# First attention of a two-block transformer kernel: a head's short score units, its combinations and its exponentials moved; the last head reordered; meta scores 128 wide in the second attention

## What is computed

```python
def diff_attention(q1, q2, k1, k2, v, lam, q_chunk_blocks, k_chunk):
    def block(args):
        qb1, qb2, qc = args
        mask = k_chunk[None, :] <= qc[:, None]
        def probs(qb, k):
            s = jnp.einsum('bqhd,bkhd->bhqk', qb, k).astype(jnp.float32) * scale
            return jax.nn.softmax(jnp.where(mask, s, -jnp.inf), axis=-1)
        a = probs(qb1, k1) - lam * probs(qb2, k2)
        return jnp.einsum('bhqk,bkhd->bqhd', a.astype(v.dtype), v)
...
    o = rms_norm(o, g_sub) * (1.0 - lam_init)
    return h + o.reshape(B, L, H * DIFF_V_DIM) @ w_o
```

## Time and profile before

| | |
|---|---|
| median of 3 runs | 2028.45 us (2028.07 to 2030.13) |
| time of the profiled execution | 2028.63 us |
| its span, first to last instruction | 2026.8 us |
| PE busy | 2009.0 us, 99% |
| DVE, ACT, POOL busy | 1317.6, 852.0, 1164.9 us |
| granted TensorE clock | 0.999 of full speed (2.4 GHz) |
| first attention, heads 0 to 7, about | 30 to 251 us of the span |
| second attention, about | 718 to 863 us |

### The profile page before, as it was taken

One profiled execution on the slowest core, in us unless ns is written; L12 is line 12 of the kernel. 1 busy time (PEld: TensorE's weight loads), 2 busy tenths in 40 slices (PEclk: granted clock), 3 DMA queues, 4 the chain that ended last, 5 costly groups with the idle time before them and its releaser, 6 DMA issues.

```text
span 2026.8 us, 37421 instructions
## 1 busy us (share of the span) xinstructions
PE 2009.0 (99%) x13376; PEld 1804.8 (89%) x13376; DVE 1317.6 (65%) x2199; ACT 852.0 (42%) x1499; POOL 1164.9 (57%) x1395
## 2 busy tenths in 40 slices
PE   9999999999999999999999999999999999999998
PEld 9999899999999988899999998777788888988987
DVE  7777757857746868757857778865512457857654
ACT  5444434433423577634433425344422234433433
POOL 6445356675757522146675767744455557766765
PEclk9999999999999999999999999999999999999999
DMA  5222122232233311122232323322223223232322
GB/s 190 84 74 72 53 85 92 84 117 92 92 97 115 94 34 42 32 89 94 67 131 94 104 94 105 104 84 83 74 93 103 84 84 95 83 125 83 125 83 84
DMA packets 51986, 183.06 MB, mean 90 GB/s; under 512 B 5648, under 2 KB 7824, under 8 KB 51856
## 3 DMA queue, kind: packets, MB, share of 16 engines
q1 hardware_dynamic: 50304, 178.87, 27.3%
q10 hardware_dynamic: 1552, 2.42, 0.4%
HBM read 179.17 MB, written 2.10 MB: 89 GB/s over the span
## 4 chain that ended last, share of the span: by engine, by line
PE 93%; DVE 4%; issue 1%; ACT 1%; POOL 1%; DMA 0%; DVEq 0%; ACTq 0%; SPq 0%
PE ps L805 25%; PE ps L806 24%; PE ps L807 24%; PE ps L929 3%; PE ps L930 3%; PE ps L931 3%; PE ps L1180 2%; PE ps L1197 1%; PE ps L1190 1%; PE ps L1090 1%; PE ps L1121 1%; POOL w_lo L759 1%; PE ps L1105 0%; PE ps L1191 0%; PE ps L1407 0%
## 5 line engine op out<-in xcount | busy, mean ns | idle before, releaser
L739 POOL TENSOR_TENSOR w_lo<-w_raw,w_hi 128x256 fp32r<-128x256 f32 x1140 | 964.1, 878 | 744.5 <-ACT w_hi L2256 735.9
L805 PE MATMUL ps<-x_hi,w_hi 128*128 128x264 f32 (+2 forms) x2504 | 823.0, 329 | 0.0
L806 PE MATMUL ps<-x_lo,w_hi 128*128 128x264 f32 (+2 forms) x2504 | 813.5, 325 | 0.0
L807 PE MATMUL ps<-x_hi,w_lo 128*128 128x264 f32 (+2 forms) x2504 | 812.3, 324 | 0.0
L805 PEld LDWEIGHTS ps<-x_hi,w_hi 128*128 128x128 f32 x2504 | 471.3, 188 | 49.6 <-issue 5.4
L806 PEld LDWEIGHTS ps<-x_lo,w_hi 128*128 128x128 f32 x2504 | 470.8, 188 | 42.1 <-issue 0.2
L807 PEld LDWEIGHTS ps<-x_hi,w_lo 128*128 128x128 f32 x2504 | 471.3, 188 | 39.6
L2256 ACT ACTIVATE w_hi<-w_raw 128x1024 fp32r<-128x1024 f32 x267 | 278.0, 1049 | 72.1 <-PE ps L807 56.4
L805 PE MATMUL ps<-g_hi,w_hi 128*128 128x264 f32 (+3 forms) x648 | 207.9, 321 | 1.0 <-DVE g_lo L1916 1.0
L806 PE MATMUL ps<-g_lo,w_hi 128*128 128x264 f32 (+3 forms) x648 | 205.9, 318 | 0.0
L807 PE MATMUL ps<-g_hi,w_lo 128*128 128x264 f32 (+3 forms) x648 | 205.6, 317 | 0.0
(11 more groups left out here) (278 smaller groups left out, 3044.1 us busy)
## 6 DMA issues: line engine op xcount, KB each, us to landing
w_raw<-stream SPq DMA_DIRECT2D x334, 512.0 KB, 3.5
h<-x_t SPq DMA_DIRECT2D x4, 528.0 KB, 6.7
out_t<-h SPq DMA_DIRECT2D x6, 256.0 KB, 2.3
scratch<-rotary_tables ACTq DMA_DIRECT2D x4, 264.0 KB, 5.4
out_t<-h ACTq DMA_DIRECT2D x2, 256.0 KB, 2.5
par<-params ACTq DMA_DIRECT2D x1, 342.0 KB, 4.7
scratch<-positions ACTq DMA_DIRECT2D x1, 256.0 KB, 2.6
cst<-shape_constants ACTq DMA_DIRECT2D x1, 193.0 KB, 6.2
```

The costliest lines, as they stand in the source:

```text
L739: last = nc.gpsimd.tensor_tensor(w_lo[:, ring(j), cols], w_raw[:, j % 4, cols], w_hi[:, ring(j), cols].bitcast(F32), ALU.subtract)
L805: nc.tensor.matmul(out_ap, w_hi[:, s, c], xh[:, k, cols], start=first, stop=False)
L806: nc.tensor.matmul(out_ap, w_hi[:, s, c], xl[:, k, cols], start=False, stop=False)
L807: return nc.tensor.matmul(out_ap, w_lo[:, s, c], xh[:, k, cols], start=False, stop=last)
```

## The change

1. PE: `scores` 1 to 4 of head `hd + 1` leave the start of `head_a(hd + 1)` and stand at the end of `head_a(hd)`, ahead of `sub_sum` and `value_transposes`.
2. ACT: `exps(hd + 1, 1)` leaves the start of the next head and stands ahead of `take_values(hd + 1)`.
3. DVE: `combine` and `piece_a` stand ahead of the norm step of the same idx. The order at the end of the head (`maximum` 0, p5, `take_output` 4, `combine` 0) is kept.
4. Last head: other order of `wo_blocks`, `sub_sum` and, on DVE and ACT, of norms and copies; `sub_sum` uses banks 2 and 5. `tile_pair` gets `held=1`, so only the last block of both tiles is left for it (before: one block of the first and two of the second).
5. Second attention: unit 4's scores take 128 query columns instead of 16 as stationary operand. The other 112 rows of the result aren't read.

```diff
@@ tile_pair
-                        for b in range(blocks - 1 - m, blocks):
+                        for b in range(blocks - (held if m else 1), blocks):
@@ scores_of_b
-                s = scores_b(idx)
+                s = scores_b(idx) if t else ps[:, 4, UNIT_COLS[2] + UNIT_COLS[3]:UNIT_COLS[2] + UNIT_COLS[3] + META]
...
-                    last = nc.tensor.matmul(s[:, k0:k1], q_b[rows, h % 4, q0:q0 + nq], k_b[rows, h % 4, k0:k1],
+                    last = nc.tensor.matmul(s[:, k0:k1], q_b[rows, h % 4, q0:q0 + P], k_b[rows, h % 4, k0:k1],
@@ PE head_a
-                for idx in range(1, 5):
-                    step(scores, idx)
                 for idx in range(5):
...
+                for idx in range(1, 5):
+                    scores(hd + 1, 1 - par_, idx)
                 if sums:
-                    sub_sum(hd - 1, 1 - par_, 0, 6 * hd + 11)
+                    sub_sum(hd - 1, 1 - par_, (0, 1), 6 * hd + 11)
                 value_transposes(hd + 1, 1 - par_)
@@ PE last_head_a
-                for idx in range(1, 5):
-                    scores(hd, par_, idx)
                 transposes(hd, par_, 0)
-                sub_sum(HEADS_A - 2, 0)
+                pe.wait_ge(ln_done, N_SUB + HEADS_A - 2)
+                wo_blocks(0, 0, 0, 5)
                 values(hd, par_, 0)
+                pe.wait_ge(exp_done, 5 * hd + 2)
+                sub_sum(HEADS_A - 2, 0, (2, 5))
                 transposes(hd, par_, 1)
-                pe.wait_ge(ln_done, N_SUB + HEADS_A - 1)
-                wo_blocks(0, 0, 0, 5)
+                wo_blocks(0, 1, 0, 5)
                 values(hd, par_, 1)
                 transposes(hd, par_, 2)
-                wo_blocks(0, 1, 0, 5)
+                wo_blocks(0, 0, 5, 6), wo_blocks(0, 1, 5, 6)
                 values(hd, par_, 2)
                 transposes(hd, par_, 3)
-                wo_blocks(0, 0, 5, 6), wo_blocks(0, 1, 5, 6)
+                wo_blocks(0, 0, 6, 7), wo_blocks(0, 1, 6, 7)
                 values(hd, par_, 3)
                 transposes(hd, par_, 4)
-                wo_blocks(0, 0, 6, 7), wo_blocks(0, 1, 6, 7)
+                pe.wait_ge(ln_done, N_SUB + HEADS_A - 1)
+                wo_blocks(1, 0, 0, 2)
                 values(hd, par_, 4)
                 pe.wait_ge(exp_done, 5 * HEADS_A)
                 pe.wait_ge(r_ready, N_SUB + HEADS_A - 1)
-                wo_blocks(1, 0, 0, 3)
-                sub_sum(HEADS_A - 1, 1, 4)
-                wo_blocks(1, 0, 3, 6), wo_blocks(1, 1, 0, 6)
+                wo_blocks(1, 0, 2, 6)
+                sub_sum(HEADS_A - 1, 1, (4, 5))
+                wo_blocks(1, 1, 0, 7), wo_blocks(1, 0, 6, 7)
@@ DVE head_a
+                    combine(hd, par_, idx + 1)
+                    piece_a(hd + 1, 1 - par_, idx)
                     if norms and idx < 3:
                         (sub_scale, sub_hi, sub_lo)[idx](hd - 2)
-                    combine(hd, par_, idx + 1)
-                    piece_a(hd + 1, 1 - par_, idx)
                     take_output(hd, par_, idx)
@@ DVE last_head_a
+                combine(hd, par_, 1)
                 sub_scale(hd - 2)
-                combine(hd, par_, 1)
                 take_output(hd, par_, 0)
+                combine(hd, par_, 2)
                 sub_hi(hd - 2), sub_lo(hd - 2)
-                combine(hd, par_, 2)
                 take_output(hd, par_, 1)
+                combine(hd, par_, 3)
                 sub_scale(hd - 1)
-                combine(hd, par_, 3)
                 take_output(hd, par_, 2)
-                sub_hi(hd - 1)
                 combine(hd, par_, 4)
-                sub_lo(hd - 1)
+                sub_hi(hd - 1), sub_lo(hd - 1)
@@ ACT head_a
                 for idx in range(5):
+                    if idx in range(1, 4):
+                        exps(hd, par_, idx + 1)
+                    take_transposed(hd, par_, idx)
                     if idx == 4:
-                        take_transposed(hd, par_, idx)
                         exps(hd + 1, 1 - par_, 0)
-                    else:
-                        exps(hd, par_, idx + 1)
-                        take_transposed(hd, par_, idx)
...
+                exps(hd + 1, 1 - par_, 1)
                 take_values(hd + 1, 1 - par_)
```

More of the change, by code:

```diff
@@ L831, in pair_blocks, with tile_pair @@
                            b == 0, False)
-            def tile_pair(j, tl, blocks, xh, xl, T, ready, begun=False):
+            def tile_pair(j, tl, blocks, xh, xl, T, ready, begun=False, held=2):
                 if not begun:
@@ L845, in tile_pair, with tiles @@
                     last.then_inc(half_done, 1)
-            def tiles(j, tl, n, blocks, xh, xl, T, ready, after_first=None, paired=False, begun=False, T_odd=None):
+            def tiles(j, tl, n, blocks, xh, xl, T, ready, after_first=None, paired=False, begun=False, T_odd=None, held=2):
                 done = 0
@@ L855, in tiles @@
                 if paired:
-                    tile_pair(j, tl, blocks, xh, xl, T, ready, begun)
+                    tile_pair(j, tl, blocks, xh, xl, T, ready, begun, held)
                     done = 2
@@ L872, in norm_sum @@
             def norm_sum(steps, T, src=acc, semaphore=acc_step, bank0=6, pieces=0):
+                banks = bank0 if isinstance(bank0, tuple) else (bank0, bank0 + 1)
                 pe.wait_ge(semaphore, steps)
@@ L876, in norm_sum @@
                     wait(pe, chunk_taken, pieces + bank if not isinstance(pieces, int) or pieces else 0)
-                    last = nc.tensor.matmul(ps[:, bank0 + bank, 0:n], ones[:, :], src[:, t0:t0 + n],
+                    last = nc.tensor.matmul(ps[:, banks[bank], 0:n], ones[:, :], src[:, t0:t0 + n],
                                             start=True, stop=True)
@@ L1244, in head_b, with sub_sum @@
                     output_blocks(1, 1, 0, 6)
-            def sub_sum(n, par_, bank0=0, pieces=0):
+            def sub_sum(n, par_, bank0=(0, 1), pieces=0):
                 pe.wait_ge(r_ready, N_SUB + n)
@@ L1314, in _ @@
             piece_a(0, 5)
+            for idx in range(1, 5):
+                scores(0, 0, idx)
             pe.wait_ge(blocks_clear, 1)
@@ L1325, in _ @@
             last_head_a()
-            tiles(J_WO, TL_WO, KD, KD, g_hi, g_lo, T1, (g_ready, G_WO), paired=True, begun=True)
+            tiles(J_WO, TL_WO, KD, KD, g_hi, g_lo, T1, (g_ready, G_WO), paired=True, begun=True, held=1)
             ffn(J_F0, TL_F0, X_F0, G_F0, T1, N_F0, layer=0)
@@ L2319, in inverse_rms @@
                     act.wait_ge(ss_ready, norm + 1)
-                    src = ps[:, bank0, 0:T2] if T == T2 else ps[:, bank0:bank0 + 2, 0:T // 2]
+                    a, b = bank0 if isinstance(bank0, tuple) else (bank0, bank0 + 1)
+                    src = ps[:, a, 0:T2] if T == T2 else ps[:, a:b + 1:b - a, 0:T // 2]
                 else:
@@ L2460, in sub_square, with sub_rms @@
                 square(o_buf[:, n, :], par_, 0, (o_taken, 5 * n + 5), (ss_ready, N_SUB + n - 1), T1)
-            def sub_rms(n, bank0=0):
+            def sub_rms(n, banks=(0, 1)):
                 wait(act, sub_step, n)
-                inverse_rms(N_SUB + n, P, T1, acc, bank0)
+                inverse_rms(N_SUB + n, P, T1, acc, banks)
             def head_a(hd, par_, j, i=0):
@@ L2489, in last_head_a @@
                 hd, par_ = HEADS_A - 1, 1
-                exps(hd, par_, 1)
                 take_transposed(hd, par_, 0)
[L2492 to L2495, removed]
+                exps(hd, par_, 2)
+                sub_rms(hd - 1, (2, 5))
+                take_transposed(hd, par_, 1)
+                exps(hd, par_, 3)
+                take_transposed(hd, par_, 2)
+                exps(hd, par_, 4)
+                take_transposed(hd, par_, 3)
                 take_transposed(hd, par_, 4)
@@ L2611, in _ @@
             hi_part(6)
+            exps(0, 0, 1)
             take_values(0, 0)
@@ L2621, in _ @@
             sub_square(HEADS_A - 1, 1)
-            sub_rms(HEADS_A - 1, 4)
+            sub_rms(HEADS_A - 1, (4, 5))
             residual(J_WO, TL_WO, T1, N_F0)
```

## The result

| | before | after |
|---|---|---|
| median of the timed runs | 2028.3 us | 2056.3 us |
| span of the profiled execution | 2026.8 us | 2055.7 us |
| PE busy | 2009.0 us | 2018.6 us |
| granted TensorE clock, mean | 0.999 | 0.992 |

The account below looks back on a forecast made before the run. The prediction took PE, busy 99% of the span, as the bound; 5.4 + 9.05 + 2.34 + 0.3 - 2.4 = +14.7 us on 2028.45 gave 2043.2 us, range 2038 to 2047.5.

Parts of the forecast that it names:

- Between two heads: Head transitions: transposes 0 begin 2.34 us later, hole of 0.63 at transposes 1 goes; +14.45 over seven, +2.34 into the last.
- Chain: From p5 taken to transposes 0: combination 0, maximum 1, exponentials of unit 1, copy of the values; 5.72 us.
- The point on DVE's list: DVE does maximum 1 only behind combination 0, so the exponentials and ACT's copy of the values wait.
- Rival (d): TensorE's clock falls behind holes of over 2 us, next piece at 1.2 GHz: +23, 2066 us; chance 0.02.
- The sum: All terms: 5.4 + 9.05 + 2.34 + 0.3 - 2.4 = +14.7 us, giving 2043.2 us.
- Meta scores: Second attention, unit 4's wide scores: step falls from 0.64 to 0.48 us in 15 heads, -2.4 us (at worst +1.8).
- the drain: Meta scores: the 0.22 us in front of the narrow pair agrees with an engine drain on changing tiling mode.
- The last head: Last head: old holes go, new ones come at w_o's blocks and the end; +0.3 us, ends -2 and +2.
- The hole at blocks 6: Last head: w_o's blocks 6 wait for sub_hi and sub_lo of head 6 on DVE; 2.3 us.
- DVE's order: DVE's combinations and pieces ahead of norms: pieces taken at most 0.7 us earlier, no gain beyond 0.63 at transposes 1.
- Rival (a): Copy of the values not late between heads, other holes won: -9.9, 2018.5 us; chance 0.05.
- Rival (b): Combination 0's 1.11 us step partly a clash that goes, 0.45 less in eight transitions: -3.6, 2038 us; chance 0.10.

Follow-up runs that it names:

- e2: Changed kernel with dummy matmuls on PE behind scores 1 to 4 (6 a head, 10 where there is no sum), results unused: 2046.1 us, ratio 1.0084.
- e5: Changed kernel with maximum 1 ahead of combination 0 on DVE between two heads: 2045.4 us, ratio 1.0089.
- e7: Kernel before with the changed last head alone (scores 1 to 4 and exponentials of unit 1 stay at its start, held=1): 2030.5 us, ratio 1.0008.
- e8: Kernel before with DVE's combine and piece_a ahead of the norms (not in the last head) and meta scores 128 wide: 2024.6 us, ratio 0.998.
- e6: e1 with PE's value transposes also ahead of the sum: 2029.2 us, ratio 0.9999.
- e1: Changed kernel with ACT's copy of the values and the norm ahead of the exponentials of unit 1 again: 2032.7 us, ratio 1.002.
- e9: e6 with w_o's blocks reordered around the last sum in the last head, and scores 3 and 4 behind value transposes in heads 0 and 1: 2026.6 us, ratio 0.9987.

## Where the prediction was right and where it failed

- **Between two heads**: right, step by step. Chain 5.69 against 5.72; hole put down to the copy; no hole at transposes 1; period 29.73 against 29.7, once the clock is held at full (e2), and 29.64 where it stayed at full by itself. The point on DVE's list holds as well: half a microsecond of the chain went with maximum 1 moved (e5).
- **The clock**: this is the step that failed. The sum has no term for it: new holes of 2.3 us and more were priced as delay alone, and the clock was left at full speed. Rival (d) had the mechanism, but a chance of 0.02, because the last head's hole of 1.18 had left the clock at 1.00. That row says nothing of holes twice as long. The rival's price was too high too: +23 for a fall behind every hole and through all of the next piece. The trace shows seven falls, the first twice as long as the others: behind the holes at transposes 0 of heads 1 to 5 and 7, not of heads 0 and 6, and one more within the last head. e2, which removed the six at transposes 0, puts their cost at 10 us. The sum is then 14.7 forecast, 10 for these falls, and 3 that e2 still lies above the forecast (1.6 for the meta scores, 1.4 in the last head): 28. Here the Trainium skill (TensorE: Matmul & The Clock Gate, Part 1) was right that idleness sends the clock back to half rate; the trace agrees.
- **Meta scores**: sized wrong, -2.4 against -0.8. The step itself became shorter, 0.64 to 0.52 us from unit 3's second matmul to the third transpose, where 0.48 was forecast. But "PE shows hardly a wait" was read as room, where ACT's copy was just in time in every second head. The rule of the Trainium skill on column tiling (TensorEngine Tiling (Array Packing), Performance Considerations, "When to Use Tiling") did not decide here: the wide form is the faster. Of the 0.12 us, 0.09 lie ahead of the pair, where the prediction saw the drain; that it is one is not shown.
- **The last head**: +0.3 against +0.8 in e7, at full clock. The hole at blocks 6 was forecast at 2.3 and is 2.12. In the changed kernel the same stretch is 3.0 us longer than before (61.5 against 58.5): the clock falls twice in it, which the forecast left out.
- **DVE's order**: "nothing is gained beyond the 0.63 counted" was right, but the gain was put down to both moves. e8 shows that this order alone closes the holes, so the move of the scores had nothing to win there.
- **Rival (a)**, the faster side, did not come; e6 with the copy hidden is level with before, 11 us above its 2018.5. Most of that is, by e6's trace, the last head (60.7 us, where the rival wanted 2.5 less than 58.5: 4.7), the holes of heads 0 and 1 (2.0), the Ln (1.4) and the meta scores (1.6).
- **Rival (b)**, a shorter chain, did not come either: the last step of combination 0 took 1.11 us again. In e5 it took 0.77, with 0.66 instead of 0.50 for the step ahead of it; why isn't shown.

## What to carry to other kernels

When independent work is moved out from between a producer and its consumer, look at what it hid: here 1.7 us of scores covered a copy of 0.74. When a step is put ahead of another in an in-order engine's list, add up the chain behind its wait, on every engine. And price a hole on TensorE twice, as delay and as clock: the rows before can only acquit holes of the length that they show.

## What the runs showed of the hardware

The granted clock can drop from 2.4 to 1.2 GHz even in a kernel whose PE is busy 98% of the whole span (231.8 of 256 us in the stretch of these falls). Holes of 0.8 to 1.1 us at transposes 0 (e1 and e2, eight each) were followed by no fall; of the eight of 1.7 to 2.8 us in e5, two were; of the eight of 2.3 to 3.4 in the changed kernel, six were. Length alone does not decide in that range: in the changed kernel no fall followed the hole of 3.19 in head 0. One and the same hole of 2.12 us in the last head was followed by a fall in the changed kernel, e1, e2, e5 and e6, but not in e7; nor did one follow the 2.20 in e9. What does decide stays open, and each of these kernels has one trace only. Behind such a fall a piece took 4.0 to 5.2 us instead of 3.0.

Dummy matmuls in such holes were worth their place: six or ten of them a head took 10 us off. A stationary operand of 16 columns between ones of 128 cost 0.12 us more than a wide one: it begins 0.22 us behind the matmul ahead of it, against 0.12 with the wide one. The load of the narrow one took 0.09 us, against 0.19.
